# A decoder trunk in fp32 halves: one pass over five token blocks, or two phases with seven half-depth products for gate and up

## What is computed

```python
proj = rmsnorm(x) @ w_in + b_in            # 1024 x (3*512 conv + 4*512 mLSTM + 8 gates)
x += concat(short_conv(...), mlstm(...)) @ w_out
x += cross_attn(rmsnorm(x), mem_k, mem_v)  # 256 memory rows, 4 heads of 256
g, u = split(rmsnorm(x) @ w_gu)            # 1024 x 2*2816
x += (silu(g) * u) @ w_down                # 2816 x 1024
y = rmsnorm(x)
```

## Time and profile before

| | us |
|---|---|
| median of 3 runs | 2899.18 (2897.5 to 2899.67) |
| profiled execution, span | 2896.7 |
| TensorE matmul busy | 2856.6 (99%) |
| VectorE / ScalarE / GpSimd busy | 1189.9 / 753.1 / 431.2 |
| DMA | 801 MB, mean 277 GB/s |

### The profile page before, as it was taken

The page is one execution under the profiler, slowest core; times in us unless marked ns, Lnnn a source line. Parts: engine busy times, 40 slices in busy tenths (PEclk is TensorE's granted clock), DMA queues, the critical chain, the costliest instruction groups (busy, mean ns, idle before and its releaser), DMA issues.

```text
span 2896.7 us, 38358 instructions
## 1 busy us (share of the span) xinstructions
PE 2856.6 (99%) x15739; PEld 2694.2 (93%) x15739; DVE 1189.9 (41%) x2258; ACT 753.1 (26%) x1467; POOL 431.2 (15%) x284
## 2 busy tenths in 40 slices
PE   8899999999999999999999999999999999999998
PEld 7788888888899999999999999999999999999998
DVE  7735655323533344233334547434332242442123
ACT  5443343232332220113222110322211023221001
POOL 2643444444310000001000102000000000000000
PEclk9999999999999999999999999999999999999999
DMA  7887778788685788768687889967567777666675
GB/s 265 317 342 279 290 259 293 291 287 310 242 305 207 268 305 303 267 240 328 224 301 289 318 322 398 359 240 260 213 234 274 262 263 281 224 246 248 255 267 186
DMA packets 144998, 801.14 MB, mean 277 GB/s; under 512 B 15949, under 2 KB 31693, under 8 KB 65081
## 3 DMA queue, kind: packets, MB, share of 16 engines
q1 hardware_dynamic: 119216, 719.10, 67.1%
q0 software_dynamic: 16208, 67.87, 6.7%
q10 hardware_dynamic: 9400, 11.72, 1.2%
HBM read 650.30 MB, written 148.33 MB: 276 GB/s over the span
## 4 chain that ended last, share of the span: by engine, by line
PE 93%; DMA 3%; DVE 3%; issue 1%; ACT 1%; ACTq 0%; POOL 0%; SPq 0%; DVEq 0%; POOLq 0%
PE gb L628 82%; PE gb L872 3%; PE ta L872 2%; PE td L872 1%; DMA big<-kd_d 1%; DMA w_hl<-split_d 1%; PE ta L738 0%; DVE act_lo L1427 0%; DMA big<-rows_d 0%; DVE xn_lo L1398 0%; DMA made_d<-big 0%; DVE big L1392 0%; PE gm L854 0%; DMA w_raw<-w_kv 0%; PE ta L736 0%
## 5 line engine op out<-in xcount | busy, mean ns | idle before, releaser
L628 PE MATMUL gb<-xn_hi,w_hl 128*128 128x384 f32 (+2 forms) x5800 | 1581.9, 349 | 5.1 <-DVE big L1434 1.9
L628 PEld LDWEIGHTS gb<-xn_hi,w_hl 128*128 128x128 f32 x5800 | 1060.5, 188 | 53.6 <-issue 3.3
L628 PE MATMUL gb<-xn_lo,w_hl 128*128 128x384 f32 (+2 forms) x2920 | 1011.2, 346 | 0.0
L628 PE MATMUL gb<-act_hi,w_hl 128*128 128x384 f32 (+3 forms) x3184 | 846.4, 345 | 13.0 <-DVE w_hl L1403 10.9
L628 PEld LDWEIGHTS gb<-act_hi,w_hl 128*128 128x128 f32 x3184 | 579.3, 188 | 42.0 <-DVE w_hl L1403 11.2
L628 PEld LDWEIGHTS gb<-xn_lo,w_hl 128*128 128x128 f32 x2920 | 548.5, 188 | 24.0 <-issue 0.5
L628 PE MATMUL gb<-act_lo,w_hl 128*128 128x384 f32 (+3 forms) x1592 | 546.8, 343 | 0.0
L498 POOL TENSOR_TENSOR w_hl<-w_raw,w_hl 128x1024 fp32r<-128x1024 f32 x136 | 335.6, 2477 | 427.1 <-ACT w_hl L1019 427.0
L1454 DVE TENSOR_TENSOR work<-gb,r_res 128x384 f32<-128x384 f32 (+2 forms) x220 | 128.4, 586 | 581.8 <-PE gb L628 548.6
L628 PEld LDWEIGHTS gb<-act_lo,w_hl 128*128 128x128 f32 x1592 | 300.0, 188 | 12.2 <-issue 0.2
L1645 DVE TENSOR_TENSOR x<-x,gb 128x384 f32<-128x384 f32 (+2 forms) x200 | 115.6, 582 | 397.5 <-PE gb L628 394.0
(11 more groups left out here) (316 smaller groups left out, 2148.5 us busy)
## 6 DMA issues: line engine op xcount, KB each, us to landing
w_hl<-split_d SPq DMA_DIRECT2D x484, 1024.0 KB, 5.0
split_d<-w_hl SPq DMA_DIRECT2D x121, 1024.0 KB, 5.1
w_raw<-w_st SPq DMA_DIRECT2D x105, 512.0 KB, 6.3
w_raw<-w_kv SPq DMA_DIRECT2D x32, 512.0 KB, 5.5
made_d<-big ACTq DMA_DIRECT2D x32, 256.0 KB, 4.5
w_raw<-made_d SPq DMA_DIRECT2D x16, 512.0 KB, 8.0
big<-kd_d POOLq DMA_DIRECT2D x8, 1024.0 KB, 12.9
big<-vd_d POOLq DMA_DIRECT2D x8, 1024.0 KB, 12.8
```

The lines of the kernel that those rows point to most:

```text
L628: mm = pe.matmul(bank[:, 0:wd], a[:, s, k * P:(k + 1) * P], r[:, k, 0:wd], start=(first and k == ks[0] and i == 0), stop=(last and k == ks ...
```

## The change

**Two phases.** Phase one runs gates to W_XO for all five blocks. x after W_XO goes to `x_d` in memory, x scaled for the FFN to `xn_d`. Phase two is the FFN over all 2056 columns in three blocks of 688, 684 and 684, each as two halves of 344 or 342 (`FH`).

**Seven products.** For each of the 22 hidden tiles f, the gate and up weights (1024 deep, as two halves of 512) and the two token halves form a 2 x 2 by 2 x 2 block product. It is made of 7 half-depth products in place of 8, after the scheme of Strassen and Winograd: four sums of weights per f (`weight_sum`, on VectorE), four sums of inputs per block (`made_operand`). The results of products are combined in PSUM (four of them accumulate on a bank that already holds others) and by copies on ScalarE and additions on VectorE. Seven weight operands are now split in high and low for every f and block: high by ScalarE (`unit_high`), low by GpSimd for products 0, 3, 6 and for the down tiles, by VectorE for 1, 2, 4, 5. Split weights are no longer stored or reloaded in phase two; raw weights of 512 KB are loaded by SP.

**Other moves.** Down groups are `[4, 4, 4, 2, 4, 4]`. Next x is prepared during scores and XO. Rows, x and next x are transferred by SP and not GpSimd. Decode arithmetic over states and caches goes to GpSimd: a product, then a fold by halves; score pieces run in block 3, value pieces in block 4 of phase one; the decode outputs' products hook into W_OUT of block 4 at m = 5 and 7. y is stored once for each FFN block.

Constants, and which low halves GpSimd makes (a unit is one weight operand; f < 0 is a down tile):

```diff
-FFG = [8, 7, 7]
...
-DM, DO, DX = 1, 2, 3
+DM, DO, DX = 1, 2, 4
...
+NT = sum(BLK) * P + NDEC
+FT0 = [0, 688, 1372]
+FW = [688, 684, 684]
+FH = [w // 2 for w in FW]
+NFB = len(FW)
+NH = max(FH)
+FFG = [4, 4, 4, 2, 4, 4]
+NG = len(FFG)
+PRODUCTS = 7
+NU = 8
+NQ = 4
+LOOK = 5
+T_B11, T_B21, T_T4, T_B22, T_T1, T_T2, T_T3 = range(7)
+OPERAND = [T_B11, T_B21, T_T2, T_T1, T_T3, T_B22, T_T4]
...
+def pooled(u):
+    _, _, f, p = UNITS[u]
+    return f < 0 or p in (0, 3, 6)
```

TensorE, one pair and the down tiles of a group:

```diff
+def pair(b, gr, f):
+    n = FH[b]
+    j = pair_of(b, gr, f)
+    first = gr == 0 and f == 0
+    gate, low, high = bank_set(gr + f)
+    if f == 0:
+        after(pe, h_done, j)
+    else:
+        after(pe, h_done, j - 1)
+    if f == 1:
+        after(pe, evac_done, 2 * KT * group_of(b, gr))
+        if j == 1:
+            read_out(pe, G_ALL - 1)
+    for p, bank in enumerate((gate, low, gate, high, gate, high, gate)):
+        u = unit_at(b, gr, f, p)
+        if p == 2:
+            pe.wait_ge(copied, 3 * j + 1)
+        elif p == 4:
+            pe.wait_ge(copied, 3 * j + 2)
+        elif p == 5:
+            pe.wait_ge(copied, 3 * j + 3)
+        elif p == 6:
+            pe.wait_ge(c22_done, j + 1)
+        unit_ready(u)
+        if first:
+            pe.wait_ge(t_lo, 7 * b + p + 1)
+        t = OPERAND[p]
+        for k in range(4):
+            for i, (a, r) in enumerate(((0, 0), (0, 1), (1, 0))):
+                mm = pe.matmul(bank[:, 0:n], units[:, u % NU, a, k * P:(k + 1) * P], tq[:, t, r, k, 0:n],
+                               start=(p in (0, 1, 3) and k == 0 and i == 0), stop=(k == 3 and i == 2),
+                               skip_group_check=p in (2, 4, 5, 6))
...
+for m in range(2):
+    unit_ready(unit_at(b, gr, -1, m))
+    down(b, gr, m, range(size - 1), size)
+pe.wait_ge(ah_lo, j + size)
+for m in range(2):
+    down(b, gr, m, (size - 1,), size)
+for m in range(2, KT):
+    unit_ready(unit_at(b, gr, -1, m))
+    pe.wait_ge(evac_done, d + 2 * (m - 1))
+    down(b, gr, m, range(size), size)
```

ScalarE, one step for each product:

```diff
+def pair_step(u, b, gr, f, p):
+    n = FH[b]
+    j = pair_of(b, gr, f)
+    first = gr == 0 and f == 0
+    gate, low, high = bank_set(gr + f)
+    if p in (0, 2, 3):
+        act.wait_ge(product_done, FINISHED[u])
+        dst, src = {0: (sp_1, gate), 2: (sp_q, gate), 3: (sp_5, high)}[p]
+        act.activation(dst[:, 0:n], src[:, 0:n], ACT.Copy).then_inc(copied, 1)
+    unit_high(u + LOOK)
+    if p == 3 and first:
+        if b == 0:
+            rnorm(r_res, td, r_row_at(NB - 1), w_x(NB - 1))
         else:
...
+            final_norm(b - 1, r_fin_at(b - 1))
+        act.preload_act_table_set("silu_and_others")
+    if p == 1 and not first or p == 3 and first:
+        act.wait_ge(g_done, 2 * j + 1)
+        act.activation(ef[:, 0, 0:n], gf[:, 0, 0:n], ACT.Silu).then_inc(silu_done, 1)
+    if p == 5:
+        act.wait_ge(g_done, 2 * j + 2)
+        act.activation(ef[:, 1, 0:n], gf[:, 1, 0:n], ACT.Silu).then_inc(silu_done, 1)
+    if p == 6:
+        act.wait_ge(h_done, j + 1)
+        act.activation(ah[:, 0, f, :, 0:n], hf[:, :, 0:n], ACT.Copy).then_inc(ah_hi, 1)
```

VectorE, one step for each product:

```diff
+def pair_step(u, b, gr, f, p):
+    n = FH[b]
+    j = pair_of(b, gr, f)
+    gate, low, high = bank_set(gr + f)
+    if p == 0 and f:
+        hidden_low(b, j - 1, f - 1)
+    if p == 1:
+        v.wait_ge(product_done, FINISHED[u])
+        v.wait_ge(copied, 3 * j + 1)
+        v.tensor_tensor(gf[:, 0, 0:n], low[:, 0:n], sp_1[:, 0:n], ALU.add).then_inc(g_done, 1)
+    if p == 4:
+        v.wait_ge(product_done, FINISHED[u])
+        v.wait_ge(copied, 3 * j + 3)
+        v.tensor_tensor(c22[:, 0:n], gate[:, 0:n], sp_5[:, 0:n], ALU.add).then_inc(c22_done, 1)
+    if p == 5:
+        v.wait_ge(product_done, FINISHED[u])
+        v.tensor_tensor(gf[:, 1, 0:n], high[:, 0:n], sp_q[:, 0:n], ALU.add).then_inc(g_done, 1)
+    if p == 6:
+        v.wait_ge(product_done, FINISHED[u])
+        v.wait_ge(silu_done, 2 * j + 2)
+        v.wait_ge(c22_done, j + 1)
+        v.tensor_tensor(hf[:, 0, 0:n], gate[:, 0:n], ef[:, 0, 0:n], ALU.mult)
+        v.tensor_tensor(hf[:, 1, 0:n], ef[:, 1, 0:n], c22[:, 0:n], ALU.mult).then_inc(h_done, 1)
+    if gr == 0 and f in (1, 2) and p % 2 == 0:
+        m = (f - 1) * 4 + p // 2
+        if b:
+            final_scale(b - 1, m)
         else:
...
+            scale_tile(m)
```

VectorE beside the down tiles, and what each step prepares ahead:

```diff
+    evacuate(b, gr, p)
+    if gr == NG - 1:
+        if 2 <= p:
+            square_sum(b, p - 1)
+        if b < NFB - 1:
+            for i in {4: (0, 1), 5: (2, 3)}.get(p, ()):
+                made_operand(b + 1, i)
+            for i in {6: (0, 1), 7: (2, 3)}.get(p, ()):
+                operand_low(b + 1, i)
+if gr == 0 and f == 0 and p < 3:
+    operand_low(b, p + 4)
+for ahead, i in ((6, 0), (5, 1), (4, 2), (2, 3)):
+    if u + ahead < len(UNITS) and UNITS[u + ahead][2] >= 0 and UNITS[u + ahead][3] == 0:
+        weight_sum(PAIR[u + ahead], i)
+if u + LOOK - 1 < len(UNITS) and not pooled(u + LOOK - 1):
+    unit_low(u + LOOK - 1)
```

GpSimd: the fold of the decode work, and the low halves of phase two:

```diff
+def fold(src, n, out):
+    while n > 2:
+        n //= 2
+        st(pool.tensor_tensor(src[..., 0:n], src[..., 0:n], src[..., n:2 * n], ALU.add))
+        st.settle()
+    st(pool.tensor_tensor(out, src[..., 0], src[..., 1], ALU.add))
...
+for u in range(len(UNITS)):
+    if pooled(u):
+        w = unit_width(u)
+        pool.wait_ge(unit_hi_done, u + 1)
+        pool.tensor_tensor(units[:, u % NU, 1, 0:w], unit_source(u), units[:, u % NU, 0, 0:w].bitcast(F32),
+                           ALU.subtract).then_inc(unit_lo_p, 1)
```

TensorE, the waits of the decode outputs:

```diff
-t0 = 0 if m == 3 else 4
-for i in range(t0, t0 + 4):
-    pe.wait_ge(dw_loaded[(KT + i) % NR], 16 * ((KT + i) // NR) + 16)
+if m == 5:
+    pe.wait_ge(dec_pool, POOL_VALUES)
+t0 = 0 if m == 5 else 4
+pe.wait_ge(dw_loaded, 16 * (KT + (KT if t0 else NR)))
```

More of the change, by code:

```diff
@@ new lines, in _ @@
+            for g in range(G_LOW, G_ALL - 2):
+                mixer_transfers((g - G_KV) // G_BLK, (g - G_KV) % G_BLK)
+                split(g)
+            sp.wait_ge(dec_pe, PE_OUT)
+            sp.wait_ge(xn_stored, 32 * (NB - 1))
+            for i in range(4):
+                operand(0, i)
+            for q in range(3):
+                ffn_weights(q)
+            split(G_ALL - 2)
+            split(G_ALL - 1)
+            sp.wait_ge(pt_done, NB * 8)
+            ffn_weights(3)
+            read_out(sp, G_ALL - 1)
@@ new lines, in sum_rows, with sum_final @@
+            def sum_rows():
+                pe.wait_ge(res_acc, 18 * NB)
+                sumsq(acc_res, td, w_x(NB - 1))
+            def sum_final(b):
+                n = FH[b]
+                pe.wait_ge(fin_acc, 6 * b + 6)
+                pe.wait_ge(fin_sq, 8 * b + 8)
+                for half, bank in enumerate((tb, td)):
+                    pe.matmul(bank[:, 0:n], ones, accf[:, half, 0:n], start=True, stop=False)
+                    mm = pe.matmul(bank[:, 0:n], ones, sqf[:, half, 0:n], start=False, stop=True)
+                mm.then_inc(ssq_done, 1)
@@ new lines, in down @@
+            def down(b, gr, m, ks, size):
+                n = FH[b]
+                u = unit_at(b, gr, -1, m)
+                for half in range(2):
+                    bank = down_bank(gr, m, half)
+                    for k in ks:
+                        for i, (a, r) in enumerate(((0, 0), (0, 1), (1, 0))):
+                            mm = pe.matmul(bank[:, 0:n], units[:, u % NU, a, k * P:(k + 1) * P], ah[:, r, k, half, 0:n],
+                                           start=(k == 0 and i == 0), stop=(k == size - 1 and i == 2))
+                    if ks[-1] == size - 1:
+                        mm.then_inc(product_done, 1)
@@ L985, in _ @@
-                    for i in range(3):
-                        gemm(d + i, W, act_hi, act_lo, most, None if i else hid_wait, last=False)
-                    for i in range(3):
-                        gemm(d + i, W, act_hi, act_lo, rest, None if i else hid_wait, first=False)
-                    for m in range(3, KT):
-                        gemm(d + m, W, act_hi, act_lo, range(size))
-                    fo += size
-            W = w_ffn(NB - 1)
-            pe.wait_ge(res_acc, (NB - 1) * 27 + 26)
@@ L1701, in _ @@
                 st.settle()
-                pt0 = b * 8
+                for e in range(5, KT if b < NB - 1 else 0):
+                    next_sq(b + 1, e)
                 def score_bank(p, t):
```

1282 lines of the change are left out of this document (753 added, 529 removed).

## The result

The changed kernel takes 2929.6 us (median of 4 runs, 2925.0 to 2943.8) against 2898.3: ratio 1.0118, 95% interval 1.0094 to 1.0142. It is slower by some 31 us, where 2865 us was forecast.

What follows compares the result with a forecast made beforehand. TensorE, busy 99% of the span, was taken as the bound. 2896.7 - 110 + (3 + 6 + 5 + 8) + (7 + 12 + 7 + 16 + 3) + 9.5 = 2863, so 2865 us by the median; range 2810 to 2920.

Steps and rivals of the forecast that it cites:

- the price of a matmul: On TensorE: 0.418 ns a column plus 13 ns whatever the width, so 156.8 ns at 344 columns and 156.0 at 342.
- The end: After the last matmul: evacuation, sums, scalings and stores take 20.3 us where they took 10.8, +9.5.
- (c): Between FFN blocks: VectorE's extra work in the last four down tiles delays the next block's first products, +16 (6 to 24).
- I cost that at nothing, cover 15 us: SP's queue: DMA rows moved from GpSimd join split weights loaded six tiles ahead; no cost, 15 us of cover.
- (a): Second and third pairs of an FFN block: VectorE also scales eight tiles, 4 us a block, +12 (0 to 20).
- The holds: Blocks 2 to 4 of phase one: GpSimd's decode holds VectorE's 384-column operations in norm chain and XO, +5 (0 to 15).
- The pairs: FFN pairs: VectorE's lateness reaches TensorE at the seventh product, 0.1 us a pair over 66 pairs, +7.
- XO's scalings: Before XO's first evacuation: scaling and low parts of the next input leave TensorE without a bank in four blocks, +6.
- The two-tile group: FFN down group of two tiles: 12 matmuls, 1.9 us, ahead of a last tile whose chain takes about 4.3, +7 (3 to 10).
- The value pieces: Last block of phase one: TensorE waits at the sixth W_OUT tile for decode outputs needing 16 value pieces, +8 (0 to 39).
- GpSimd and VectorE bind the pairs: Rival for FFN pairs: three low halves on GpSimd make VectorE late every time, 13.8 us against 13.1, 2909 us; chance 0.20.
- all is covered: Rival: steady pairs, scaling and value pieces stay hidden and transitions cost half, 2812 us; chance 0.22.

Runs made afterwards that it cites:

- The first edit: Changed kernel with ScalarE's copy of the hidden units ahead of its copy of the fifth down tile's weights in each FFN block's first group: 2908.6 us.
- the version of all parts: Changed kernel with copy first, low halves early, scaling on ScalarE, transposes later, rows on ScalarE's queue, xn on multiples of 64 bytes, two-tile end stores: 2875.9 us.
- the best version: All those edits together on the changed kernel, plus product 3's low half on VectorE again: 2871.6 us, ratio 0.9906 to the kernel before.

## Why the prediction was wrong

**What held.** The bound, the price of a matmul and the count. Steady pairs stand at 156.1 ns for 342 columns (forecast 156.0) and 158.1 for 344 (156.8), down tiles at 157.3 for 342, some 6 us more in all than the sum had; and the three blocks have the 2904 products and down matmuls each that were counted, plus sums. By the other rule the prediction weighed, that of the Trainium skill (TensorE: Matmul & The Clock Gate, Back-to-back issue gap), which the section gives for an isolated matmul, 342 columns would take 145.0 ns; the trace disagrees, and its own row, was the better guide. The end (20.7 for 20.3) held, and (c), the block transitions: 13.2 us in three places where 16 in two and 3 in the third were forecast. The sum of all idle time held as well, 77 us more for 76.5, but by luck: as the terms below show, some were far too high and others far too low.

**The step that failed: the clock had no price.** Every idle time in the sum stands at its own length, and the stream at full speed all through. That is a term put at nothing, without a reason. The runs show most waits of over 2 us followed by matmuls at the lower level, 2.1 and 2.8 us in the two stretches shown. Over the span matmuls lose 31 us so, and 5 before: 26 of the 66 us. The first edit shows it too. The copy removed 13 us of waits and saved 21; its mean clock rose from 0.986 to 0.988, which over the span is worth some 6 of these 8 us.

**Addresses had none either.** Spacings were taken from a kernel whose operands lie otherwise. Over xn the changed kernel's matmuls are 3 ns slower at 384 columns and 6 to 7 at 512, some 13 us; one way of placing them gave 4.5 back. With the 6 us of the FFN's spacing and the clock that is 45 of the 65 us that busy time missed; the other 20 were not taken apart.

**A second step that failed: SP's order and queue.** "I cost that at nothing, cover 15 us" was worked out for the blocks in which split weights are loaded ahead. In block 0 SP issued the rows some 15 us after their store's issue, behind raw weight tiles, and they landed 14.7 us after that, with the engines 92% full. TensorE waited 10.1 us, and 1.3 in the kernel before; an earlier issue on another queue got some 7 us back. The same step was not made at all for the residual's load, which the change also puts on SP; with ScalarE's order behind it that was the largest single cause, 21 us.

**(a) named the wrong engine.** 12 us were charged to VectorE's final scaling in the second and third pairs. TensorE did stop, 13.4 us in three places, but two pairs later, at the first down group; the chain goes over ScalarE to a load, and VectorE was in time. The size was right by luck and the reason wrong, and the reason would have led to the wrong cure.

**The holds were undersized.** They had +5 (0 to 15) and came to 15 to 21 us of waits, over the range. The row that showed a hold of one whole GpSimd operation was right; what was missed is how short the slack is. The transposes stand 1.1 us (six matmuls) into the next head's product, and 2.6 us more takes two thirds of the wait away.

**Terms that were too high.** The pairs, +7: 0. XO's scalings, +6: no wait of TensorE names them. The two-tile group, +7: 2.5, three waits of 0.85. The value pieces, +8: 0. A piece takes 8.1 us on average (8.5 forecast), the first begins 16 us into the block and the last ends at 145 (144), but the loads behind them landed in 6.5 us median, not in the 22.3 of the earlier trace rows, which came from a fuller queue, and TensorE got there at 173 and not at 159, since it had waited elsewhere. Where those waits were cured it comes earlier, and then this one is there: 3.4 to 7.6 us in six of the variants. It was late next.

**The rivals.** That GpSimd and VectorE bind the pairs is out: 13.1 to 13.3 us, not 13.8, with two or three low halves alike. The slower outcome that it stood for came from elsewhere. The rule named with it, that of the Trainium skill (GPSIMD Engine Reference, Engine selection), held in its sign as far as these runs tell: with one low half back on VectorE the medians were 9 us lower, and 4 in the version of all parts, with overlapping intervals, and nothing changed in the steady pairs. That all is covered (2812) is out by the waits listed above. The measured time lies outside all the cases that the prediction had, since none of them priced the clock.

What stays open: phase one of the best version takes 1446.8 us, still 36.6 more than before. Its longest new waits are 4.1 us for the next block's sum, 4.4 (in two places) for the decode weights and 3.8 for the rows; the rest was not taken apart. Open too is the rule behind the addresses.

## What to carry to other kernels

When a kernel is 99% bound by one engine, a change that moves work off it also spends the slack of every order and queue beside it. List each transfer that the change moves onto a queue with what will stand right behind it there, and which engine's order has an unrelated instruction waiting for that. A wait of over 2 us mostly costs its length and the slow clock after it; give that a price in the sum. And when such a change comes out slower, follow the chain to its first link before choosing the cure: here the edits that cured it moved instructions, issues and 32 bytes, and none touched what is computed.

## What the runs showed of the hardware

- A VectorE operation between SBUF tiles that starts beside a GpSimd tensor operation can last until that one or the next ends, however small it is: 3 columns in 2.34 us (0.17 alone), a scaling of 128 columns in 2.95 (0.28 alone). That includes tensor_scalar, with one tensor as input.
- GpSimd's operations cost 1.36 us at 512 columns (1.24 forecast from half of 1024; 1.59 where they read the summed weights), 0.84 at 256, 0.55 at 128, 0.37 at 64 and 0.21 at 4: some 0.2 us each whatever the size, as this group shows of 4 columns:

```profile
L760 POOL TENSOR_TENSOR dec<-w_raw 128x4 f32<-128x4 f32 x32 | 6.6, 206 | 2.5
```

- 32 bytes in the start of a matmul's moving operand changed its spacing at 384 columns from 173 to 177 ns. At 512 and 392 columns and in the FFN the same edit gave 233 to 229, no gain and 156.1 to 158.3.
- With the 16 DMA engines over 90% full, four broadcasts of 258 KB reached their reader 11.4 us after the first issue (14.7 in another execution). Issued 9.6 us earlier on the same queue they took 16.9, and so they came 4.2 us earlier; on a queue of their own, issued earlier still, 16.7.
- A wait of TensorE of 4.4 us was followed by 24 matmuls that took 2.1 us (344 columns) and 2.8 us (342) more than at full speed, with the granted clock at 0.5 behind it.
